# The second scan of a hybrid mLSTM/GLA/MoE layer: state in two 64-row halves, new orders on three engines

## What is computed

```python
def gla_states(k, v, log_a, state):
    """S_t = diag(a_t) S_{t-1} + k_t v_t^T."""
    ...
    b = jnp.cumsum(chunk(log_a, GLA_CHUNK), axis=3)
    kv = jnp.einsum('bhnsk,bhnsv->bhnkv', kc * jnp.exp(b_end[:, :, :, None] - b), vc)
    s_new = jnp.exp(be)[..., None] * s_st + kvc
def gla_outputs(q, k, v, log_a, pre):
    ...
    inter = jnp.einsum('bhntk,bhnkv->bhntv', qc * jnp.exp(b), pre)
    att = jnp.einsum('bhntk,bhnsk,bhntsk->bhnts', qc, kc, decay)
    o = jnp.einsum('bhnts,bhnsv->bhntv', att, vc) + inter
```

## Time and profile before

| | us |
|---|---|
| median of 3 runs | 1299.09 (1297.24 to 1300.75) |
| the profiled execution's own time | 1300.56 |
| its span in the trace | 1298.8 |
| second scan, first score to last read | 512.1 to 574.2 |
| output projection and router | 575.9 to about 700 |
| experts | about 730 to the end |

### The profile page before, as it was taken

The page is one execution under the profiler, slowest core; times in us unless marked ns, Lnnn a source line. Parts: engine busy times, 40 slices in busy tenths (PEclk is TensorE's granted clock), DMA queues, the critical chain, the costliest instruction groups (busy, mean ns, idle before and its releaser), DMA issues.

```text
span 1298.8 us, 18473 instructions
## 1 busy us (share of the span) xinstructions
PE 1223.7 (94%) x6911; PEld 1049.7 (81%) x6911; DVE 930.3 (72%) x1059; ACT 766.3 (59%) x907; POOL 241.6 (19%) x170
## 2 busy tenths in 40 slices
PE   5999999999999999999994899999999999999993
PEld 3778788998989999878883888888888888888882
DVE  5757321586546632874557889999999999999986
ACT  6544330764335544953343277787777877877784
POOL 1100000110000000050000023333333333333134
PEclk9999999999999999999997999999999999999997
DMA  9871240343463213142127699999999999999994
GB/s 375 286 167 39 90 137 1 114 147 134 177 257 130 98 68 116 62 154 90 66 81 299 247 372 369 400 404 406 408 408 408 406 404 404 404 404 405 406 333 175
DMA packets 78473, 319.86 MB, mean 246 GB/s; under 512 B 7256, under 2 KB 31864, under 8 KB 48648
## 3 DMA queue, kind: packets, MB, share of 16 engines
q1 hardware_dynamic: 70480, 290.66, 56.6%
q0 software_dynamic: 7936, 28.40, 8.4%
HBM read 291.68 MB, written 35.75 MB: 252 GB/s over the span
## 4 chain that ended last, share of the span: by engine, by line
PE 82%; DVE 8%; ACT 3%; DMA 3%; issue 2%; SPq 0%; POOL 0%; POOLq 0%; DVEq 0%; ACTq 0%
PE psum L2656 36%; PE psum L2269 9%; PE psum L2592 7%; PE psum L2332 3%; PE psum L2333 3%; PE psum L2334 3%; PE psum L2365 1%; PE psum L2364 1%; PE psum L2363 1%; DVE e_lo L2034 1%; DMA xs<-x 1%; DMA raw<-w_in_units 1%; PE psum L2416 1%; PE psum L2679 1%; PE psum L2417 1%
## 5 line engine op out<-in xcount | busy, mean ns | idle before, releaser
L2034 DVE TENSOR_TENSOR e_lo<-e_raw,e_hi 128x2048 fp32r<-128x2048 f32 x192 | 432.3, 2285 | 39.3 <-ACT e_hi L1342 39.2
L1342 ACT ACTIVATE e_hi<-e_raw 128x2048 fp32r<-128x2048 f32 x192 | 365.7, 1915 | 95.7 <-PE psum L2656 94.7
L2656 PE MATMUL psum<-e_hi,xt_hi 128*128 128x512 f32 x496 | 153.4, 390 | 1.5 <-DVE e_lo L2034 0.9
L2656 PE MATMUL psum<-e_lo,xt_hi 128*128 128x512 f32 x496 | 152.9, 389 | 0.0
L2656 PE MATMUL psum<-e_hi,xt_lo 128*128 128x512 f32 x496 | 152.9, 389 | 0.0
L2656 PEld LDWEIGHTS psum<-e_hi,xt_hi 128*128 128x128 f32 x496 | 92.7, 188 | 21.6 <-DVE e_lo L2034 1.3
L2656 PEld LDWEIGHTS psum<-e_hi,xt_lo 128*128 128x128 f32 x496 | 93.1, 188 | 19.6
L2656 PEld LDWEIGHTS psum<-e_lo,xt_hi 128*128 128x128 f32 x496 | 93.1, 188 | 19.5
L846 POOL DMA_INDIRECT x_tok<-xn_dram,tok_g x56 | 102.3, 1827 | 23.8 <-issue 12.8
L2332 PE MATMUL psum<-w_hi,h_hi 128*128 128x256 f32 x352 | 100.6, 286 | 1.1 <-ACT gq L1136 1.1
L2333 PE MATMUL psum<-w_hi,h_lo 128*128 128x256 f32 x352 | 99.6, 283 | 0.0
(11 more groups left out here) (430 smaller groups left out, 2411.2 us busy)
## 6 DMA issues: line engine op xcount, KB each, us to landing
e_raw<-w_e_units SPq DMA_DIRECT2D x192, 1024.0 KB, 9.4
ada_x<-w_ada_rows SPq DMA_DIRECT2D x16, 1024.0 KB, 4.9
raw<-w_in_units SPq DMA_DIRECT2D x13, 1024.0 KB, 6.9
ada_raw<-w_ada_units SPq DMA_DIRECT2D x8, 1024.0 KB, 21.9
bc<-rows_dram SPq DMA_DIRECT2D x16, 512.0 KB, 3.8
xs<-x SPq DMA_DIRECT2D x4, 1024.0 KB, 11.7
acc_dram<-zero_r SPq DMA_DIRECT2D x1, 4096.0 KB, 20.2
wo_raw<-w_out SPq DMA_DIRECT2D x4, 1024.0 KB, 6.1
```

The costliest lines, as they stand in the source:

```text
L1342: act.activation(e_hi[u % EH][:], e_raw[u][:], ACT.Copy).then_inc(e_hi_ok, 1)
L2034: dve.tensor_tensor(e_lo[u][:], e_raw[u][:], e_hi[u % EH][:], ALU.subtract).then_inc(e_lo_ok, 1)
L2656: m = pe.matmul(o[:, BANK * b:BANK * (b + 1)], x[:, k, :], w[:, D * j + BANK * b:D * j + BANK * (b + 1)], start=a, stop=z)
```

## The change

- State and g_ps are kept as 64-row halves: g_ps is [P, 2, 2, HD], head h on partitions 64h to 64h+63. The state product (in the scan and in `ctx_product`) is four products of 128 columns, two with weights of 64 columns for each group, whose results lie on partitions 0 to 63 and 64 to 127. `scaled_state` is two activations on 128 partitions, the add has 256 columns.
- The read takes qz times g_ps as four 64-row products. Heads h = 0 and h = 1 write different banks (third and fourth of the direction), and the state lies in the upper half of the fourth bank. `gla_out` reads both banks (`by_parity`).
- `g_state` waits in addition for og_done of its own step, which is the copy of that step's output.
- qz and k_tok have four buffers (l % 4).
- TensorE's step: scores of l+1, state product of l-1, transposes of l+2, read of l. ScalarE's: exponentials of l+3, keys of l+2, carry of l-1, wo_hi. VectorE's: output of l-1, keys of l+2, mask of l+1, add of l-1, queries of l+2, wo_lo. Ahead of the loop ScalarE has keys of 0, exponentials of 2, keys of 1; TensorE has the transposes of 1.
- `yt_ps(0, .)` lies in banks 0 and 1 instead of 2 and 6.

```diff
-        g_ps = at("g_ps", AT_OUT + 58 * KB, [P, 2, 2, 2 * HD])
+        g_ps = at("g_ps", AT_OUT + 60 * KB, [P, 2, 2, HD])
...
+        def gla_out_ps(d):
+            v = psum[:, BANK * (4 * d + 2):BANK * (4 * d + 4)].rearrange("p (x n) -> p x n", x=2)
+            return v[:, :, 0:2 * HD].rearrange("p x (i n) -> p x i n", i=2)
+
+        def gla_state_ps(d):
+            return gla_bank(d, 3, 512)[:, 2 * HD:4 * HD]
...
-            b = (2, 6)[a] if s == 0 else 6 + a
+            b = a if s == 0 else 6 + a
...
-                at_least(act, gkv_mm, l - 1)
-                act.activation(k_tok[d], gla_bank(d, 1, 2 * P).rearrange("p (i t) -> p i t", i=2), ACT.Copy).then_inc(gkh_ready, 1)
+                at_least(act, gkv_mm, l - 3)
+                act.activation(k_tok[l % 4], gla_bank(d, 1, 2 * P).rearrange("p (i t) -> p i t", i=2), ACT.Copy).then_inc(gkh_ready, 1)
...
-                    for h in range(2):
-                        q, v = slice(64 * h, 64 * h + 64), slice(HD * h, HD * (h + 1))
-                        x = act.activation(g_ps[q, d, i, v], src[q, 2 * HD * i + HD * h:2 * HD * i + HD * (h + 1)], ACT.Copy,
-                                           scale=gcol[q, 4, 2 * d + i, c:c + 1])
+                    x = act.activation(g_ps[:, d, i, :], src[:, HD * i:HD * (i + 1)], ACT.Copy, scale=gcol[:, 4, 2 * d + i, c:c + 1])
...
             gla_keys(0)
+            gla_exps(2)
+            gla_keys(1)
             for l in range(2 * TL):
-                if l + 1 < N_STATE:
-                    gla_keys(l + 1)
-                if l + 2 < 2 * TL:
-                    gla_exps(l + 2)
+                if l + 3 < 2 * TL:
+                    gla_exps(l + 3)
+                if l + 2 < N_STATE:
+                    gla_keys(l + 2)
+                if 1 <= l <= N_STATE:
+                    gla_carry(l - 1)
                 if 1 <= l < 9:
                     wo_hi_part(l - 1)
-                if 1 <= l <= N_STATE:
-                    gla_carry(l - 1)
...
-                at_least(dve, go_mm, l - 1)
-                dve.tensor_tensor(qz[d], gq[:, :, ds(P * (c - TC), P)], e_q[d], ALU.mult).then_inc(gx_ready, 1)
+                at_least(dve, go_mm, l - 3)
+                dve.tensor_tensor(qz[l % 4], gq[:, :, ds(P * (c - TC), P)], e_q[d], ALU.mult).then_inc(gx_ready, 1)
...
             for l in range(2 * TL):
-                if 2 <= l + 1 < 2 * TL:
-                    gla_qz(l + 1)
                 if l >= 1:
                     gla_out(l - 1)
-                if 1 <= l <= N_STATE:
-                    gla_add(l - 1)
                 if l + 2 < 2 * TL:
                     gla_kx(l + 2)
                 if l + 1 < 2 * TL:
                     gla_scores(l + 1)
+                if 1 <= l <= N_STATE:
+                    gla_add(l - 1)
+                if l + 2 < 2 * TL:
+                    gla_qz(l + 2)
                 if 2 <= l < 10:
                     wo_lo_part(l - 2)
...
+            def state_product(o, k, c):
+                for i in range(2):
+                    for h in range(2):
+                        q = slice(64 * h, 64 * h + 64)
+                        x = pe.matmul(o[q, HD * i:HD * (i + 1)], k[:, i, q], gv[:, c, HD * (2 * i + h):HD * (2 * i + h + 1)],
+                                      start=True, stop=True)
+                return x
...
             def g_state(l):
                 d, c = gla_step(l)
                 pe.wait_ge(gkh_ready, l + 1)
+                pe.wait_ge(og_done, l + 1)
                 at_least(pe, ps_ready, l - 1)
-                for i in range(2):
-                    x = pe.matmul(gla_bank(d, 2, 4 * HD)[:, 2 * HD * i:2 * HD * (i + 1)], k_tok[d][:, i, :],
-                                  gv[:, c, 2 * HD * i:2 * HD * (i + 1)], start=True, stop=True)
-                x.then_inc(gkv_mm, 1)
+                state_product(gla_state_ps(d), k_tok[l % 4], c).then_inc(gkv_mm, 1)
...
                 for i in range(2):
-                    o = gla_bank(d, 3, 512)[:, 2 * HD * i:2 * HD * (i + 1)]
-                    pe.matmul(o, qz[d][:, i, :], g_ps[:, d, i, :], start=True, stop=False)
+                    for h in range(2):
+                        q = slice(64 * h, 64 * h + 64)
+                        pe.matmul(gla_out_ps(d)[:, h, i, :], qz[l % 4][q, i, :], g_ps[q, d, i, :], start=True, stop=False)
                     for h in range(2):
                         v = slice(HD * (2 * i + h), HD * (2 * i + h + 1))
-                        x = pe.matmul(o[:, HD * h:HD * (h + 1)], g_a[d][:, 2 * i + h, :], gv[:, c, v], start=False, stop=h == 1)
+                        x = pe.matmul(gla_out_ps(d)[:, h, i, :], g_a[d][:, 2 * i + h, :], gv[:, c, v], start=False, stop=True)
...
             pair_out(pe, PAIRS["r1"][0] + 3)
+            g_transposes(1)
             pe.wait_ge(ctx_out, 6)
             for l in range(2 * TL):
-                if l + 1 < N_STATE:
-                    g_transposes(l + 1)
-                if l < N_STATE:
-                    g_state(l)
                 if l + 1 < 2 * TL:
                     g_scores(l + 1)
+                if 1 <= l <= N_STATE:
+                    g_state(l - 1)
+                if l + 2 < N_STATE:
+                    g_transposes(l + 2)
                 g_read(l)
```

More of the change, by code:

```diff
@@ L234, in build @@
         g_a = [stage(2 + d).rearrange("p (h t) -> p h t", h=NH) for d in range(2)]
-        qz = [g_qz[:, d, :, :] for d in range(2)]
+        qz = [g_qz[:, j, :, :] for j in range(4)]
         kx = [g_kx[:, d, :, :] for d in range(2)]
-        k_tok = [g_kt[:, d, :, :] for d in range(2)]
+        k_tok = [g_kt[:, j, :, :] for j in range(4)]
         e_q = [g_e[:, d, 0, :, :] for d in range(2)]
@@ L1794, in gla_out @@
                 if first_visit(d, c):
-                    dve.tensor_copy(og(c - TC), gla_bank(d, 3, 512)).then_inc(og_done, 1)
+                    dve.tensor_copy(by_parity(og(c - TC)), gla_out_ps(d)).then_inc(og_done, 1)
                 else:
-                    dve.tensor_tensor(og(c - TC), og(c - TC), gla_bank(d, 3, 512), ALU.add).then_inc(og_done, 1)
+                    dve.tensor_tensor(by_parity(og(c - TC)), by_parity(og(c - TC)), gla_out_ps(d), ALU.add).then_inc(og_done, 1)
                 if TL < l < 2 * TL - 2:
@@ L1868, in ctx_state @@
                 dve.wait_ge(ctx_out, 2 + d + 1)
-                dve.tensor_tensor(ctx_ps, ctx_ps, g_ps[:, d, :, :].rearrange("p i n -> p (i n)"), ALU.add).then_inc(ctx_add, 1)
+                v = ctx_ps[:, 0:2 * HD]
+                dve.tensor_tensor(v, v, g_ps[:, d, :, :].rearrange("p i n -> p (i n)"), ALU.add).then_inc(ctx_add, 1)
             ctx_state(0)
```

17 lines of the change are left out of this document (8 added, 9 removed).

## The result

The changed kernel takes 1309.75 us (median of 7 runs, 1303.53 to 1316.77) against 1299.05 (1297.24 to 1300.78): ratio 1.0093, 95% interval 1.0071 to 1.0116 (the ratio is an estimate from all runs of both kernels and not the quotient of the medians, which is 1.0082). It is slower; the forecast was 1301.0 with 1295.5 to 1306.0. The profiled execution took 1309.75, its span is 1308.0 us, 9.2 more than before.

A forecast was written before the change was run, and what follows sets the result against it. TensorE's path was taken as the bound. Scan + 2.6, memset - 0.43 and context products - 0.3 made + 1.9 us: 1302.5 for the profiled execution, which lay 1.5 above the median, so forecast 1301.0, range 1295.5 to 1306.

The forecast's parts named there:

- Step work: TensorE's work in one scan step: 22 slots plus seven changes of shape, 3.74 us against 3.68 before.
- rival 1: Loads behind changes in short blocks are hidden, 1294.3 us; further end, changes without any price, some 1287; together chance 0.13.
- rival 2: Column halves don't run side by side in f32, 1307.3 us, chance 0.07; second form, 0.05 per slot, 1303.8, chance 0.02.
- The wait for the output copy: In each scan step TensorE's state product waits for VectorE's copy of the previous output: 0.26 us, bounds nothing to 0.5.
- Rival 3: VectorE's output copy begins late or is slower, so TensorE stands 0.5 us instead of 0.26: 1304.6 us, chance 0.18.
- Steps 10 and 11: Scan steps where head sums stand ahead of the keys, making transposes 0.35 us later each, + 0.7 in all.
- steps 12 and 13: Scan steps without transposes, 3.63 us each.
- Scores of 1 behind the table load: At the scan's start, scores of 1 wait for keys delayed by table load and exponentials, starting at 514.91 us.
- Ahead of the scan: Memset of half-size g_ps takes about 0.48 us, gaining 0.43 in TensorE's wait; four context products gain 0.3 in all.
- The start: Scan's first step: exponentials of 2 and table load before keys of 1, so step 0 ends at 517.98 against 516.50 us.
- its own forecast of 1302.5: Whole kernel, profiled execution: 1300.56 us before would become 1302.5, from a sum of + 1.9 us.
- The carry's 0.14 to 0.2 us of wait: State product's wait for ScalarE's carry in each old scan step, 0.14 to 0.2 us, which goes with the change.

The follow-up runs named there:

- fill: Changed kernel plus seven unused identity products on TensorE while it waits for the keys of step 1: 1301.92 us, ratio 1.0012.
- reordered read: Changed kernel with seven filling products, read ordered state of pair 0, scores of pairs 0 and 1, state of pair 1: 1298.34 us, ratio 0.9994.
- the halves in the old orders: Changed kernel's layouts, buffers and halved products, with the kernel before's orders on TensorE, ScalarE and VectorE: 1294.38 us, ratio 0.9955.
- Early exponentials: Changed kernel with ScalarE's exponentials of step 2 moved ahead of the last piece of the long read, no filling: 1302.21 us, ratio 1.0020.
- the split read: Changed kernel, read products with pair 0's state moved up behind the scores: 1292.94 us; with seven filling products 1291.13; with keys of 1 before exponentials of 2, 1292.05.

## Why the prediction was wrong, point by point

- Step work: forecast 3.74, measured 3.73. Column halves and row halves run side by side, there are seven changes, and none is free: rival 1 and both forms of rival 2 are out. A change costs 0.17 where the two read blocks are joined (fill against reordered read), less than the 0.20 I used as a mean; the sum was right since I had priced each by its kind.
- The wait for the output copy: forecast 0.26, measured 0.23 to 0.25. Rival 3 is out. Step 3.98 against 4.00. Steps 10 and 11: 4.27 and 4.28 against 4.35; steps 12 and 13: 3.61 each against 3.63.
- Scores of 1 behind the table load: forecast 2.80 us after the first ones (514.91 less 512.11), measured 2.86.
- The scan with the clock held (fill): + 2.1 us against + 2.6 forecast; the fill's time, 1.3 above before beside it, against + 1.9.
- Ahead of the scan, where these rows answer:

```profile
466.83 0.48 DVE L1866 MEMSET g_ps<- 128x512 f32 x1 [0.17 <-DVE modc L1865]
...
470.04 0.63 PE L2462 MATMUL psum<-ident,b_ctx 128*128 128x128 f32 x4 [0.62 <-ACT gate_rows L1201]
```

The memset takes 0.48, as forecast, but TensorE's wait behind it fell by 0.77 (1.39 to 0.62), not 0.43; the context products - 0.3, as forecast. The rest isn't the change's: from the memset's end to the transposes it is 2.7 us in both traces, and VectorE came to the memset 0.35 us earlier against TensorE, behind instructions that both kernels share.
- **The step that failed** is "The start", with the term behind it: "The scan from there: steps 1 to 11, 44.0 + 0.7". I had worked out that TensorE would stand idle there, close behind another wait, and booked the delay alone. The sum took every later duration from rows at full clock; the half-clock stretch behind the waits was put at nothing, without a reason. The trace had a warning: the kernel before has half-clock stretches elsewhere (3.4 us at 95.6, 23.9 at 696.3, 20.9 at 1280.0), none in the scan. In the profiled execution the stretch of 17.1 us costs 6.6 us (70.8 us of scan against the fill's 64.2), in the medians 7.8 (1309.75 against 1301.92). That it is the clock is shown: the fill leaves the delay and every step as they are and takes the half clock and the 6.6 us away. What makes the clock fall is known only in part: the clock held in every profile whose start has the 0.83 us wait alone or with one of 0.21 (the kernel before, the halves in the old orders, the three with the fill), and behind the two long waits the loss depends on the steps. Early exponentials nearly remove it (1302.21), the split read shortens it (1292.94 with the same waits).
- The profiled execution against its own forecast of 1302.5, 7.3 over: + 6.6 for the clock, + 3.2 for the late weight split near 1257, - 0.5 for the scan's own length, - 1.6 for what lies ahead of 464 us and - 0.4 for the memset. The 3.2 and the 1.6 are no part of the change.
- Smaller slips: the chances of a slower result add up to 0.32 (0.27 and 0.05), not 0.30. The carry's 0.14 to 0.2 us of wait a step is not what the earlier trace rows says (0.5 us in two waits); the forecast step is added up from blocks and doesn't need it.
- None of the rivals had this mechanism. 1309.75 lies past rival 2's 1307.3, but that number came from another mechanism, which the step of 3.98 rules out.

What stays open: why the clock came back after 17.1 us in one profiled execution of the changed kernel and after 37.5 in another, and why the kernel before with 2.07 us of wait kept it while the one with 1.77 did not in its profiled execution. All these kernels load weights by DMA during the start (81% of the DMA engines' time in after's 508.2 to 514.3). That load is not enough to bring the fall: the DMA share was 1.06 within the 2.07 us wait of the kernel that kept its clock. Whether it has a part in it wasn't tried.

## What to carry to other kernels

When a reorder makes TensorE wait, price the wait twice: its length, and a possible stretch behind it at half clock, with the steps behind it taken from the kernel as it will be. Its length can't be forecast from these runs (none to 37.5 us), so give it a chance and a range. Count changes of shape as work (0.17 to 0.20 us each here): halving a product gains only if it stands next to blocks of its own shape. The same halves gave + 0.9% in one order, nothing clear with the read reordered (- 0.1%), and - 0.4 to - 0.7% in others; and before you remove work that lies between two waits for another engine, look for what it covered: half of a 0.34 us gain came back as a wait.

## What the runs showed of the hardware

- The granted clock fell to 0.50 behind or within waits of 0.83 and 1.77 us in all five profiles that have them and stayed there from 3.4 to 37.5 us, by the program that ran behind them and by the execution. It fell once behind 0.83 and 0.57 us, held twice behind the same, and held behind 0.83 and 2.07 us with 2 us of work between. With seven filling products in the wait it was 1.00 in all three profiles.
- While the clock was low TensorE looked fully busy (17.10 of 17.10 us), with 94 records done where it does 148 at full clock. Busy time alone doesn't show the loss; the granted clock beside it does.
- f32 products with 64 columns of weights run in pairs side by side, as 64-row ones do: eight in four slots, 0.45 us (the state product's 0.58 to the next block holds that and the change).
- A block behind one of its own kind of shape pays no change: scores 0.45 us between two 64-row blocks, 0.65 elsewhere.
